# State advance of the running sequences placed between the convolution's matmul units, with four state buffers and the state transfers on GpSimd's queue

## The chip, the cores and the metric

The kernel runs on one core of one Trainium2 chip. The metric is the device time of one execution in microseconds (us), the median of the runs shown. One core has five engines with a queue each: PE (TensorE, matmuls), DVE (VectorE), ACT (ScalarE), POOL (GpSimd) and SP (SyncE, which here only starts transfers). They are ordered among each other by semaphores alone. The kernel is written without a scheduler: each engine executes its own hand-written list, and an instruction that waits for a semaphore holds up everything behind it on its engine.

## The reference

One step of a hybrid decoder layer, in float32: RMSNorm, a wide projection (`xn @ w_in`), two mixers side by side, sigmoid gates, an output projection, and a mixture of experts with a final RMSNorm. It runs for a new prompt of 512 tokens (`SEQ`) and for 8 running sequences (`DB`) of 8 new tokens each, 64 tokens (`ND`), 576 tokens in all (`T`).

One mixer is a short convolution of width 3 over `cc * ch`, multiplied by `cb`. The other is gated linear attention (GLA) with 4 heads (`H`), key width 128 and value width 256: `S = diag(a_t) S + k_t^T v_t`, `o_t = q_t S`. The prompt starts at a zero state. Each running sequence has a state of its own, `state_gla`, 4 x 128 x 256 floats, 512 KB: it is read, used for the sequence's 8 outputs, advanced by its 8 tokens, and returned in `gla_sample_new`. "State advance" below means this.

## The kernel before, in words

Every large matrix product is done in three passes of half-width floats (high times high, high times low, low times high). A weight group of 1 MB is loaded by SP into one of two buffers `raw`, copied by ACT to `wh` (`high`, line 703), and DVE computes the rest `wl` (`low`, line 1040). PE then works it off in units. A feature unit (`feature_unit`, matmuls at line 1585) is 48 matmuls of 288 columns and fills one of two pairs of PSUM banks; ACT or DVE empties a pair and signals `unit_free`. Groups are numbered: 8 to 11 gate the GLA output and are interleaved with the prompt's four GLA blocks, 12 to 17 (`G_CONV` to `G_GA`) are the convolution's, 18 to 21 and 22 to 25 the sigmoid gates (stage GA, then GB). Each convolution group has two units, twelve in all. A group's load waits until the low part of the group two before it is done; its `high` waits until PE has used up that group (`w_used`).

Behind the fourth GLA block of the prompt come the running sequences. PE transposes their keys (line 1696) and makes the scores (1698). It waits for ACT's copy of the keys (`kt`, line 836, behind the prompt's last `normed_output`), adds the scores' part of the output in banks 6 and 7 (line 1704), and then, sequence by sequence, does two things:

- the output's part from the state: 4 heads `qm x s0` (line 1710), when the state has been loaded (`st_load`);
- the state's increment: 4 heads `ksm x v` (line 1718) into banks 4 and 5, when POOL has masked the keys of this sequence (`km_ready`, line 568) and DVE has used the increment before (`st_ready`).

DVE computes the new state from the old one and the increment, in place (line 1235, 4 instructions). SP stores it (439) and, when the store has landed, loads the state of three sequences later into the same buffer (442): there are three buffers, `s0a`, `s0b` and `S`, the last of which also holds the prompt's state. SP's list has all of this ahead of the weight loads from group 14 on. When all is done, ACT normalises the outputs of the running sequences (`normed_output(NPT)`: four squares at line 809, POOL's power at 572 to 574, four scalings at 807). Only then do ACT and DVE go to the convolution: ACT copies `cc` (849), DVE multiplies by `ch` into `up` and `ud` (1253 to 1255), applies the taps (1263 to 1267), multiplies by `cb` (1277) and splits the result (1281). PE's list has the convolution's twelve units directly behind the last increment.

## Time and profile before

| | before |
|---|---|
| runs | 1057.36, 1057.85, 1051.64 us |
| median | 1057.36 us |
| span of the profiled execution, first to last instruction | 1039.5 us |
| PE busy | 900.2 us, 87% of the span |
| DVE, ACT, POOL busy | 53%, 43%, 21% |
| mean granted clock of PE | 0.928 of full speed |
| chain of work that ended last | PE 66%, DMA 12%, DVE 7%, POOL 5%, ACT 4% |

The page gives the profiled execution's span and no other time of it; the span is 17.9 us below the median of the runs, which includes what lies before the first and behind the last instruction. Full speed of PE is 2.4 GHz and the other level 1.2 GHz: a granted clock of 1.00 is the first, 0.50 the second, and a value between them is a mean over a stretch with both. Times of rows are microseconds from the span's start. A busy PE is not a PE at its peak.

### The profile page before, as it was taken

To read this page: it belongs to the slowest core of one execution; us is meant where nothing else is said; L and a number is where in the kernel's file an instruction comes from. 1 tells how busy PE (TensorE), PEld (TensorE's weight loads), DVE (VectorE), ACT (ScalarE), POOL (GpSimd) and SP (SyncE) were. 2 spreads that over 40 slices of the span, in tenths; PEclk is the share of its full clock that TensorE was granted. 3 is DMA by queue.
4 is the path that set the end of the run, shared out by engine and by line. 5 is a ranking of instruction groups with operands and counts; after the bars stand their busy time and mean duration, and the time that the engine had idled before them with its cause. 6 is when DMAs were issued, how large, how long until landed. Compare 5 with 4: busy or idle time off the path is not lost.

```text
span 1039.5 us, 16432 instructions
## 1 busy us (share of the span) xinstructions
PE 900.2 (87%) x6334; PEld 846.3 (81%) x6334; DVE 547.9 (53%) x695; ACT 446.5 (43%) x556; POOL 220.6 (21%) x286
## 2 busy tenths in 40 slices
PE   4999989998899999999998996269899989989950
PEld 3998988996589999999998996268888888878840
DVE  5413324655315431114654234647878878878737
ACT  5324323453021133223222124047778777778732
POOL 2000000001300000000000015215455454454533
PEclk9899989998999999999998996579999999999985
DMA  7222211112552222222434513169999999999526
GB/s 221 82 81 82 61 61 41 42 41 82 172 172 82 81 82 81 83 81 82 148 106 134 190 62 129 64 229 318 356 348 361 339 350 350 356 327 338 188 66 224
DMA packets 135535, 173.91 MB, mean 167 GB/s; under 512 B 10579, under 2 KB 120659, under 8 KB 134917
## 3 DMA queue, kind: packets, MB, share of 16 engines
q1 hardware_dynamic: 129556, 161.51, 46.7%
q0 software_dynamic: 5936, 11.81, 3.3%
q8 instruction: 30, 0.49, 0.2%
q14 instruction: 13, 0.10, 0.0%
HBM read 163.29 MB, written 17.86 MB: 174 GB/s over the span
## 4 chain that ended last, share of the span: by engine, by line
PE 66%; DMA 12%; DVE 7%; POOL 5%; ACT 4%; issue 4%; POOLq 0%; SPq 0%; ACTq 0%; DVEq 0%
PE ps L1585 51%; DMA xg<-moe_rows,curs 9%; PE ps L1845 5%; POOL curs L621 2%; DVE wl L1379 1%; ACT yb L955 1%; PE ps L1836 1%; PE ps L1675 1%; PE ps L1710 1%; POOL curd L634 1%; DMA xin<-x_sample 1%; DMA gla_sample_new<-s0b 1%; DMA s0b<-state_gla 1%; PE ps L1718 1%; PE ps L1689 1%
## 5 line engine op out<-in xcount | busy, mean ns | idle before, releaser
L1379 DVE TENSOR_TENSOR wl<-raw,wh 128x2048 fp32r<-128x2048 f32 x90 | 203.1, 2282 | 1.1 <-ACT wh L917 1.1
L1040 DVE TENSOR_TENSOR wl<-raw,wh 128x2048 fp32r<-128x2048 f32 x36 | 82.9, 2302 | 200.6 <-ACT wh L703 200.5
L1585 PE MATMUL ps<-xh,wh 128*128 128x288 f32 x832 | 180.7, 299 | 3.8 <-ACT hist L794 2.0
L1585 PE MATMUL ps<-xl,wh 128*128 128x288 f32 x832 | 179.3, 297 | 0.0
L1585 PE MATMUL ps<-xh,wl 128*128 128x288 f32 x832 | 179.3, 297 | 0.0
L917 ACT CAST wh<-raw 128x2048 fp32r<-128x2048 f32 x93 | 174.8, 1907 | 7.0 <-PE ps L1845 7.0
L1845 PE MATMUL ps<-wh,gx 128*128 128x256 f32 x512 | 140.3, 308 | 1.5 <-DVE gx L1483 1.5
L1585 PEld LDWEIGHTS ps<-xh,wh 128*128 128x128 f32 x832 | 135.3, 190 | 4.7 <-issue 2.3
L1585 PEld LDWEIGHTS ps<-xh,wl 128*128 128x128 f32 x832 | 135.2, 190 | 0.0
L1585 PEld LDWEIGHTS ps<-xl,wh 128*128 128x128 f32 x832 | 135.1, 190 | 0.0
L1845 PE MATMUL ps<-wl,gx 128*128 128x256 f32 x512 | 133.4, 295 | 0.0
L1845 PEld LDWEIGHTS ps<-wh,gx 128*128 128x128 f32 x512 | 104.5, 204 | 4.0 <-issue 1.7
L1845 PEld LDWEIGHTS ps<-wl,gx 128*128 128x128 f32 x512 | 104.8, 205 | 0.0
L703 ACT CAST wh<-raw 128x2048 fp32r<-128x2048 f32 x36 | 68.6, 1904 | 50.2 <-PE ps L1585 50.2
L556 POOL TENSOR_SCALAR ms<-ss 128x1 f32<-128x1 f32 (+2 forms) x19 | 7.3, 385 | 311.2 <-ACT v L809 230.4
L621 POOL COPY curs<-slots 64x1 int32 (+1 forms) x34 | 54.8, 1612 | 25.8 <-DVE slots L1461 19.4
L577 POOL IOTA io<- 128x160 f32 x1 | 0.3, 293 | 261.5 <-PE ps L1585 261.5
L634 POOL COPY curd<-slotd 64x1 int32 (+1 forms) x32 | 26.2, 819 | 127.5 <-ACT yb L955 127.5
L1585 PE MATMUL ps<-wh,xh 128*128 128x256 f32 x160 | 46.8, 293 | 6.6 <-ACT v L789 6.6
L1585 PE MATMUL ps<-wh,mh 128*128 128x256 f32 x160 | 46.7, 292 | 3.5 <-DVE ml L1339 3.5
L955 ACT COPY yb<-ps 64x1024 f32<-64x1024 f32 x32 | 32.2, 1007 | 35.2 <-PE ps L1585 35.2
L1585 PE MATMUL ps<-wl,mh 128*128 128x256 f32 x160 | 46.4, 290 | 0.0
(311 smaller groups left out, 1588.2 us busy)
## 6 DMA issues: line engine op xcount, KB each, us to landing
raw<-w_gate SPq DMA_DIRECT2D x32, 1024.0 KB, 6.3
raw<-w_up SPq DMA_DIRECT2D x31, 1024.0 KB, 7.7
raw<-w_down SPq DMA_DIRECT2D x30, 1024.0 KB, 7.6
raw<-w_in SPq DMA_DIRECT2D x26, 1024.0 KB, 5.1
raw<-w_gla_out SPq DMA_DIRECT2D x4, 1024.0 KB, 4.8
raw<-w_o SPq DMA_DIRECT2D x4, 1024.0 KB, 4.9
y<-moe_results SPq DMA_DIRECT2D x4, 1024.0 KB, 8.1
xin<-x_prompt SPq DMA_DIRECT2D x4, 512.0 KB, 6.5
```

The lines of the kernel that those rows point to most:

```text
L621: c(pool.tensor_copy(curs[p][:, :], slots[:, bass.ds(e, 1)]))
L634: c(pool.tensor_copy(curd[p][:, :], slotd[:, bass.ds(e, 1)]))
L703: copy(wh[par][:, :], raw[par][:, :]).then_inc(hi_ready, 1)
L917: copy(wh[m0 % 3][:, :], src[:, :]).then_inc(hi_ready, 1)
L955: copy(yb[e0 % 2][:, :].rearrange("p (a c) -> p a c", a=2), ps[0:B, 2:4, :]).then_inc(yb_ready, 1)
L1040: tt(wl[par][:, :], raw[par][:, :], wh[par][:, :].bitcast(F32), ALU.subtract).then_inc(lo_ready, 1)
L1379: tt(wl[m0 % 3][:, :], (raw[(m0 + 2) % 6] if m0 < NX else rawx[m0 - NX])[:, :], wh[m0 % 3][:, :].bitcast(F32), ALU.subtract).then_inc(lo_r ...
L1585: last.append(mm(out, left(a, k), right(b, k, o), start=k == 0 and n == 0, stop=k == k_tiles - 1 and n == 2))
L1675: ins = mm(ps[0:w, TB, q0:q0 + CH], kiv[:, hd, off:off + w], ql[:, hd, CH * n:CH * (n + 1)], start=True, stop=True)
L1689: ins = mm(ps[:, TB + hd // 2, (hd % 2) * DV:(hd % 2 + 1) * DV], kt[:, hd, :], v[:, j, hd * DV:(hd + 1) * DV], start=True, stop=True)
L1710: ins = mm(ps[0:ND, UB + hd // 2, (hd % 2) * DV:(hd % 2 + 1) * DV], qm[:, s, hd, :], s0[s % 3][:, hd, :], start=False, stop=s == DB - 1, s ...
L1845: ins = mm(ps[:, bank, 0:DE], gx[p][:, k, :], w[a][:, k, :], start=k == 0 and a == 0, stop=k == KD - 1 and a == 1)
```

## The change

The state advance is no longer a stage of its own. On PE the part from the scores is issued behind the first convolution unit, and the state advance of sequence s behind unit s + 2 (counted from 1), so that one stands behind each of the units 2 to 9. DVE's updates are spread over its convolution work in the same manner. ACT's `normed_output(NPT)` moves behind the convolution. There are four state buffers, in places that are free by then, and `up`, `ud` and `cs` are moved. The sixteen state transfers leave SP's queue and go to POOL's, between its maskings of the keys; SP's next weight load stands directly behind the store of the prompt's state.

```diff
+NS0 = 4
...
-        s0 = [sb("s0a", [P, H, DV], at=zone_b - 4 * H * DV), sb("s0b", [P, H, DV], at=zone_z + 4 * H * DV), S]
+        s0 = [sb("s0a", [P, H, DV], at=s1 + 4 * H * P), sb("s0b", [P, H, DV], at=zone_b - 4 * H * DV), S,
+              sb("s0d", [P, H, DV], at=qg_at)]
...
-        up = sb("up", [P, H, SEQ + 2])
         assert place[0] <= zone_b
+        up = sb("up", [P, H, SEQ + 2], at=zone_a)
         ud = sb("ud", [P, H, DB, DS + 2])
-        cs = sb("cs", [P, H, 2 + 2 * DB])
-        assert place[0] <= zone_b
+        assert place[0] <= s1
...
@@ block.sync
             sp.wait_ge(s_ready, NPT + 1)
             sp.dma_start(gla_prompt_new[0, 0].rearrange("h d v -> d h v"), S[:, :, :]).then_inc(out_done, 16)
-            for s in range(2):
-                if s == 0:
-                    sp.wait_ge(sg_ready, 2 * NPT + 1)
-                sp.dma_start(s0[s][:, :, :], st_in[s]).then_inc(st_load[s], 16)
-            sp.wait_ge(out_done, 16)
-            sp.dma_start(s0[2][:, :, :], st_in[2]).then_inc(st_load[2], 16)
-            for s in range(DB):
-                sp.wait_ge(st_ready, s + 1)
-                sp.dma_start(st_out[s], s0[s % 3][:, :, :]).then_inc(st_store, 16)
-                if s + 3 < DB:
-                    sp.wait_ge(st_store, 16 * (s + 1))
-                    sp.dma_start(s0[s % 3][:, :, :], st_in[s + 3]).then_inc(st_load[s % 3], 16)
             for g in range(G_CONV + 2, G_GA):
@@ block.gpsimd
-            pool.wait_ge(kt_ready, NPT + 1)
-            for s in range(DB):
+            def state_in(s):
+                pool.dma_start(s0[s % NS0][:, :, :], st_in[s]).then_inc(st_load[s % NS0], 16)
+
+            def state_out(s):
+                pool.wait_ge(st_ready, s + 1)
+                pool.dma_start(st_out[s], s0[s % NS0][:, :, :]).then_inc(st_store, 16)
+
+            def one_sequence(s):
                 if s >= 2:
                     pool.wait_ge(dkv_full, s - 1)
                 pool.tensor_scalar(ksm[s % 2][0:ND, :, :], kt[0:ND, :, :], inseq[:, s:s + 1], None,
                                    ALU.mult).then_inc(km_ready, 1)
+            pool.wait_ge(scans_done, NPT + 1)
+            state_in(0)
+            pool.wait_ge(s_ready, NPT + 1)
+            pool.wait_ge(sg_ready, 2 * NPT + 1)
+            state_in(1)
+            pool.wait_ge(out_done, 16)
+            state_in(2)
+            pool.wait_ge(kt_ready, NPT + 1)
+            one_sequence(0)
+            one_sequence(1)
+            pool.wait_ge(p1_full, NPT + 1)
+            pool.wait_ge(gla_in, NPT + 2)
+            state_in(3)
+            for s in range(DB):
+                state_out(s)
+                if s + 2 < DB:
+                    one_sequence(s + 2)
+                if s + NS0 < DB:
+                    pool.wait_ge(st_store, 16 * (s + 1))
+                    state_in(s + NS0)
...
@@ block.scalar
-            act.wait_ge(o_full, 1)
-            act.wait_ge(dkv_full, DB)
-            normed_output(NPT)
-
-            act.wait_ge(st_store, 16 * DB)
+            act.wait_ge(sg_ready, 2 * NPT + 1)
             for t in range(2):
...
+            act.wait_ge(o_full, 1)
+            normed_output(NPT)
+            act.wait_ge(cs_ready, 1)
+            act.wait_ge(st_store, 16 * DB)
             for g0, base, dst in ((G_GA, U_GA, m1), (G_GB, U_GB, sgb)):
@@ block.vector
-            for s in range(DB):
+            def state_update(s):
                 dve.wait_ge(dkv_full, s + 1)
-                dve.wait_ge(st_load[s % 3], 16 * (s // 3 + 1))
+                dve.wait_ge(st_load[s % NS0], 16 * (s // NS0 + 1))
...
-            dve.wait_ge(st_store, 16 * DB)
-            dve.wait_ge(o_full, 1)
             c(dve.memset(up[:, :, 0:2], 0.0))
             c(dve.tensor_copy(ud[:, :, :, 0:2], hist[:, :, :].rearrange("p c (s w) -> p c s w", w=2)))
+            state_update(0)
             for t in range(2):
...
                         low((g0 + 1) % 2, (g0 + 1) // 2 + 1)
+                    if t == 0:
+                        state_update(u + 1)
+                    elif u == 0:
+                        state_update(7)
...
                     tt(zl[:, ct, :], tmp[u][:, :], zh[:, ct, :].bitcast(F32), ALU.subtract).then_inc(z_ready, 1)
+                    if t == 0:
+                        state_update(u + 3)
                 low((g0 + 2) % 2, (g0 + 2) // 2 + 1)
+                if t == 0:
+                    state_update(5)
+                    state_update(6)
@@ block.tensor
+            def decode_scores():
                 ...
+            def decode_state(s):
                 ...
             for g in range(G_CONV, G_GA):
                 pe.wait_ge(lo_ready, g + 1)
                 for u in range(2):
                     free(u, N_CONV // 2 + g - G_CONV)
                     feature_unit(g % 2, u, u, X).then_inc(w_used if u else unit_full, 1)
+                    n = 2 * (g - G_CONV) + u
+                    if n == 0:
+                        decode_scores()
+                    elif n <= DB:
+                        decode_state(n - 1)
```

The bodies of `decode_scores` and `decode_state` are the instructions that stood ahead of the convolution, with the buffer number taken modulo 4 instead of 3; `decode_scores` ends with the wait for `gla_in` that stood ahead of the states.

PE's list, from the scores of the running sequences on, before (`sc`, `qm`, `bc`, `ec` are the scores, the queries of one sequence, and the two buffers of masked keys):

```order
L1698 MATMUL ps<-qg_120,ql 64x64 x4
L1704 MATMUL ps<-v,sc 64x256 [waits on_ready,sc_ready,kt_ready]
L1704 MATMUL ps<-v,sc 64x256 x3
L1710 MATMUL ps<-s0a,qm 64x256 [waits st_load0,gla_in]
L1710 MATMUL ps<-s0a,qm 64x256 x3
L1718 MATMUL ps<-v,bc 128x256 [waits km_ready]
L1718 MATMUL ps<-v,bc 128x256 x3
L1710 MATMUL ps<-s0b,qm 64x256 [waits st_load1]
L1710 MATMUL ps<-s0b,qm 64x256 x3
L1718 MATMUL ps<-v,ec 128x256 [waits st_ready,km_ready]
L1718 MATMUL ps<-v,ec 128x256 x3
```

All sequences stand one behind the other, and the first convolution unit (line 1585) comes behind the eighth.

The end of the first convolution unit, the scores' part, and the start of the second unit in PE's list now (line numbers are those of the changed kernel: 1611 is the unit, 1731 the scores' part):

```order
L1611 MATMUL ps<-xh,wl_83 128x288 x2
L1731 MATMUL ps<-v,sc 64x256 [waits on_ready,sc_ready,kt_ready]
L1731 MATMUL ps<-v,sc 64x256 x3
L1611 MATMUL ps<-xh,wh_81 128x288 [waits unit_free1,gla_in]
L1611 MATMUL ps<-xh,wh_81 128x288
L1611 MATMUL ps<-xl,wh_81 128x288 x2
```

The end of the second unit, the first sequence, and the start of the third unit now (1738 and 1746 are the former 1710 and 1718):

```order
L1611 MATMUL ps<-xl,wh_81 128x288 x2
L1611 MATMUL ps<-xh,wl_83 128x288 x2
L1738 MATMUL ps<-s0a,qm 64x256 [waits st_load0]
L1738 MATMUL ps<-s0a,qm 64x256 x3
L1746 MATMUL ps<-v,bc 128x256 [waits km_ready]
L1746 MATMUL ps<-v,bc 128x256 x3
L1611 MATMUL ps<-xh,wh_82 128x288 [waits unit_free0,lo_ready]
L1611 MATMUL ps<-xh,wh_82 128x288
L1611 MATMUL ps<-xl,wh_82 128x288 x2
L1611 MATMUL ps<-xh,wl_84 128x288 x2
```

Between two sequences there is now always one unit of 48 matmuls; the waits in front of the instructions are the same ones.

SP's list before, from the store of the prompt's state:

```order
L430 DMA gla_prompt_new<-S 128x4x256 [waits s_ready]
L434 DMA s0a<-state_gla 128x4x256 [waits sg_ready]
L434 DMA s0b<-state_gla 128x4x256
L436 DMA S<-state_gla 128x4x256 [waits out_done]
L439 DMA gla_sample_new<-s0a 128x4x256 [waits st_ready]
L442 DMA s0a<-state_gla 128x4x256 [waits st_store]
L439 DMA gla_sample_new<-s0b 128x4x256 [waits st_ready]
L442 DMA s0b<-state_gla 128x4x256 [waits st_store]
```

All but the first of these rows, and nine more like them, are gone from SP's list. POOL's list at the same place of the program now (556 loads, 560 stores, 565 masks the keys):

```order
L556 DMA s0a<-state_gla 128x4x256 [waits scans_done]
L556 DMA s0b<-state_gla 128x4x256 [waits sg_ready,s_ready]
L556 DMA S<-state_gla 128x4x256 [waits out_done]
L565 TENSOR_SCALAR bc<-kt,inseq 64x512 [waits kt_ready]
L565 TENSOR_SCALAR ec<-kt,inseq 64x512
L556 DMA s0d<-state_gla 128x4x256 [waits gla_in,p1_full]
L560 DMA gla_sample_new<-s0a 128x4x256 [waits st_ready]
L565 TENSOR_SCALAR bc<-kt,inseq 64x512 [waits dkv_full]
L556 DMA s0a<-state_gla 128x4x256 [waits st_store]
L560 DMA gla_sample_new<-s0b 128x4x256 [waits st_ready]
L565 TENSOR_SCALAR ec<-kt,inseq 64x512 [waits dkv_full]
L556 DMA s0b<-state_gla 128x4x256 [waits st_store]
```

A store, a masking and a load of a later sequence take turns, each with its wait, on one queue.

## Rows read from the trace of the kernel before

**Rows 1.** Bounds, length; busy PE, PEld, DVE, ACT, POOL; granted clock, DMA share, GB/s.
```profile
247.00:295.00 48.00, 39.89 (x150) 23.70 (x148) 16.59 (x35) 5.39 (x14) 13.66 (x10) 0.86 0.55 173
295.00:372.00 77.00, 77.00 (x578) 76.91 (x578) 31.77 (x56) 16.94 (x24) 1.22 (x2) 1.00 0.33 104
```

**Rows 2.** The chain of waits in the state advance: start, length, what.
```profile
252.47 3.67 PE ps L1704 x8
...
260.95 1.87 PE ps L1710 x8
...
275.07 3.55 PE ps L1710 x8
...
293.24 1.92 PE ps L1718 x8
```

**Rows 3.** Waits of PE from 225 to 480: total, times, longest.
```profile
PE ps L1710 <- DMA s0a<-state_gla: 2.1, 2, 1.5
PE ps L1710 <- DMA s0b<-state_gla: 2.0, 1, 2.0
```

**Rows 4.** PE's timeline: start, length, instruction, in brackets idle time before it.
```profile
249.22 0.60 PE L1696 MATMUL ps<-ident,kst 128*64 128x128 f32 x4 [1.84 <-DVE S L1215]
249.75 0.68 PE L1698 MATMUL ps<-qg,ql 128*64 128x64 f32 x8
...
285.86 3.42 PE L1710 MATMUL ps<-s0a,qm 128*64 128x256 f32 x8 [1.48 <-DMA s0a<-state_gla]
```

**Rows 5.** ACT's timeline: outputs normalised, first convolution unit emptied, first two of GA.
```profile
295.26 0.38 ACT L809 ACTIVATE v<-ps 64x256 f32<-64x256 f32 x1 [41.05 <-PE ps L1718]
...
298.23 1.55 ACT L807 ACTIVATE v<-ps,rs 64x256 f32<-64x256 f32 x4 [1.42 <-POOL rs L574]
...
301.84 0.64 ACT L849 COPY tmp<-ps 128x576 f32<-128x576 f32 x1 [2.06 <-PE ps L1585]
...
378.66 1.28 ACT L696 ACT_TABLE_LOAD   x1 [3.20 <-PE ps L1585]
...
385.07 0.20 ACT L696 ACTIVATE gnh<-gnh 128x1 f32<-128x1 f32 x1 [2.94 <-PE ps L1585]
```

**Rows 6.** The chain of waits among GLA blocks: units of 48 matmuls.
```profile
205.17 6.38 PE ps L1585 x48
...
214.63 6.47 PE ps L1585 x48
```

**Rows 7.** Busy time and granted clock in three short stretches, columns as in rows 1.
```profile
252.00:258.00 6.00, 5.53 (x13) 2.79 (x14) 2.66 (x1) 2.21 (x2) 3.12 (x2) 0.50 0.73 247
274.00:280.00 6.00, 4.92 (x15) 2.85 (x16) 0.72 (x2) 0.00 (x0) 0.68 (x1) 0.72 0.58 178
506.00:508.00 2.00, 0.39 (x3) 0.15 (x2) 1.42 (x3) 1.81 (x2) 0.00 (x0) 1.00 0.00 0
```

**Rows 8.** DVE's timeline: a convolution unit's first step, its low part, a state update.
```profile
314.66 0.46 DVE L1253 TENSOR_TENSOR up<-ps,tmp 128x288 f32<-128x288 f32 x1 [13.21 <-PE ps L1585]
...
318.30 2.29 DVE L1040 TENSOR_TENSOR wl<-raw,wh 128x2048 fp32r<-128x2048 f32 x1
...
291.24 1.65 DVE L1235 SCALAR_TENSOR_TENSOR s0a<-s0a,eb,ps 128x256 f32<-128x256 f32 x4 [5.17 <-PE ps L1718]
```

**Rows 9.** POOL's transfers: durations in ns (min/median/max) and landing; masking the keys.
```profile
L624 POOL DMA_INDIRECT xg<-moe_rows,curs x34: 955/967/1080, 675.0 to 995.5; - x34
L600 POOL DMA_DIRECT2D moe_rows<-x x5: 533/600/827, 620.2 to 633.5; - x5
...
DMA to landing us min/median/max: 2.9/3.1/5.5
...
261.05 1.56 POOL L568 TENSOR_SCALAR bc<-kt,inseq 64x512 f32<-64x512 f32 x1 [5.41 <-PE ps L1718]
```

**Rows 10.** POOL's timeline: the same power alone, and beside DVE's work.
```profile
622.59 0.56 POOL L558 TENSOR_TENSOR rs<-ms,expo 128x1 f32<-128x1 f32 x1
...
626.78 1.49 POOL L558 TENSOR_TENSOR rs<-ms,expo 128x1 f32<-128x1 f32 x1
```

More of the change, by code:

```diff
@@ L198, in build @@
         ec = sb("ec", [P, H, P])
+        qg_at = place[0]
         qg0 = sb("qg0", [P, H, P])
@@ L221, in build @@
         sgb = sb("sgb", [P, KD, T])
-        up = sb("up", [P, H, SEQ + 2])
         assert place[0] <= zone_b
+        up = sb("up", [P, H, SEQ + 2], at=zone_a)
         ud = sb("ud", [P, H, DB, DS + 2])
-        cs = sb("cs", [P, H, 2 + 2 * DB])
-        assert place[0] <= zone_b
+        assert place[0] <= s1
         h = sb("h", [P, NT, D], at=zone_v + 2 * 4 * KD * TP)
         tmp = [sb(f"tmp{i}", [P, T]) for i in range(2)]
+        cs = sb("cs", [P, H, 2 + 2 * DB])
         cso = sb("cso", [2 + 2 * DB, DC], at=zone_a + 2 * 4 * KD * T)
@@ L316, in build @@
         g_act, sg_ready = sem("g_act"), sem("sg_ready")
-        st_load = [sem(f"st_load{i}") for i in range(3)]
+        st_load = [sem(f"st_load{i}") for i in range(NS0)]
         st_store, km_ready, dkv_full, st_ready = (sem(n) for n in ("st_store", "km_ready", "dkv_full", "st_ready"))
@@ L1230, in _ @@
             low((NPT - 1) % 2, (NPT - 1) // 2 + (G_G // 2 + 1))
-            for s in range(DB):
+            def state_update(s):
                 dve.wait_ge(dkv_full, s + 1)
-                dve.wait_ge(st_load[s % 3], 16 * (s // 3 + 1))
+                dve.wait_ge(st_load[s % NS0], 16 * (s // NS0 + 1))
                 for hd in range(H):
-                    ins = stt(s0[s % 3][:, hd, :], s0[s % 3][:, hd, :], eb[:, hd, s * DS + DS - 1:s * DS + DS],
+                    ins = stt(s0[s % NS0][:, hd, :], s0[s % NS0][:, hd, :], eb[:, hd, s * DS + DS - 1:s * DS + DS],
                               ps[:, TB + hd // 2, (hd % 2) * DV:(hd % 2 + 1) * DV], ALU.mult, ALU.add)
@@ L1699, in _ @@
             ins.then_inc(p1_full, 1)
-            pe.wait_ge(kt_ready, NPT + 1)
-            pe.wait_ge(sc_ready, NPT + 1)
-            pe.wait_ge(on_ready, NPT + 1)
-            for hd in range(H):
-                mm(ps[0:ND, UB + hd // 2, (hd % 2) * DV:(hd % 2 + 1) * DV], sc[0:ND, hd, 0:ND],
-                   v[0:ND, NPT, hd * DV:(hd + 1) * DV], start=hd % 2 == 0, stop=False, skip_group_check=True)
-            pe.wait_ge(gla_in, NPT + 2)
-            for s in range(DB):
-                pe.wait_ge(st_load[s % 3], 16 * (s // 3 + 1))
+            def decode_scores():
+                pe.wait_ge(kt_ready, NPT + 1)
+                pe.wait_ge(sc_ready, NPT + 1)
+                pe.wait_ge(on_ready, NPT + 1)
+                for hd in range(H):
+                    mm(ps[0:ND, UB + hd // 2, (hd % 2) * DV:(hd % 2 + 1) * DV], sc[0:ND, hd, 0:ND],
+                       v[0:ND, NPT, hd * DV:(hd + 1) * DV], start=hd % 2 == 0, stop=False, skip_group_check=True)
+                pe.wait_ge(gla_in, NPT + 2)
+            def decode_state(s):
+                pe.wait_ge(st_load[s % NS0], 16 * (s // NS0 + 1))
                 for hd in range(H):
                     ins = mm(ps[0:ND, UB + hd // 2, (hd % 2) * DV:(hd % 2 + 1) * DV], qm[:, s, hd, :],
-                             s0[s % 3][:, hd, :], start=False, stop=s == DB - 1, skip_group_check=True)
+                             s0[s % NS0][:, hd, :], start=False, stop=s == DB - 1, skip_group_check=True)
                 if s == DB - 1:
```

## The prediction

> **What bounds the kernel here.** I read first the chain of waits of the whole execution: PE's work is 66% of it, so a change pays only where PE stands still or runs slowly. The table by stages then shows where that is near the change. In the 48 us of the state advance PE is busy 39.9 us at a mean granted clock of 0.86, although nothing in it is a large product; in the 77 us of the convolution PE is busy all the time at 1.00, DVE for 31.8 us, ACT for 16.9, POOL for 1.2, and the DMA engines a third of the time [rows 1]. The first stage is bound by waits, the second by PE with every other engine in hand.
>
> The chain of waits inside the first stage says which ones. The eight matmuls on one state take 1.87 us and the eight of its increment 1.92 when nothing is amiss; but another eight on a state take 3.55 [rows 2]. PE waited there for the loads of states, 2.0 us once and 2.1 us in two times [rows 3], and its timeline shows a second slow eight, 3.42 us, right behind an idle time of 1.48 us that ended with a load [rows 4]. So a late state costs twice, by the wait and by the lower clock level (1.2 GHz in place of 2.4) behind it. From 252 to 258 the clock stands at 0.50 without a break, and from 274 to 280 at 0.72 in the mean, that is (1 - 0.72) x 6 / 0.5 = 3.4 us at the lower level [rows 7].
>
> **What PE no longer waits for.** PE ends the scores of the running sequences at 249.75 + 0.68 = 250.43 [rows 4] and begins the first convolution unit when the last increment ends, 293.24 + 1.92 = 295.16 [rows 2]. From the first unit's copy at 301.84 to the same point of the first GA unit at 378.66 [rows 5] there are twelve units: 76.82 / 12 = 6.40 us each. The convolution thus ends at 295.16 + 76.8 = 371.96.
>
> In the changed list the first unit can start at 250.43: its weights were split during the third GLA block, and its pair of banks is free. Behind it PE has, without waits and at full clock:
>
> - twelve units, 12 x 6.40 = 76.8 us;
> - the scores' part, eight matmuls of the increment's shape but half its rows, 1.92 (it took 3.67 at the lower clock [rows 2]);
> - eight sequences, 8 x (1.87 + 1.92) = 30.3 us;
> - nine returns from small matmuls to a unit. A GLA block's unit behind small score matmuls takes 6.47 us against 6.38 behind the large ones [rows 6]: 9 x 0.09 = 0.8 us.
>
> That is 109.8 us and an end at 360.2, 11.7 us earlier than 371.96. Nothing is computed less: the 11.7 us are PE's idle time and its slow matmuls.
>
> **The gap that stays.** PE still stands for 1.84 us before it transposes the keys, since that waits for DVE's update of the prompt's state [rows 4]. Does the clock fall behind it? Gaps of 2.0 us [rows 3] and 1.48 us [rows 4] were followed by slow matmuls; from 506 to 508 PE was busy for 0.39 us of 2 and the clock stayed at 1.00 [rows 7]. In the execution shown it was at 0.50 from 252 on, though a second wait lay there too. The bounds are nothing and the 6 us of 252 to 258; matmuls there go at 1.87 / 3.55 of their speed, so it costs 6 x (1 - 0.53) = 2.8 us. I take the shorter spell, 3.4 us and 3.4 x 0.47 = 1.6, since the first slow stretch before began behind this very gap. The sum is then 11.7 - 1.6 = 10.1 us.
>
> **DVE.** It now waits for an increment between two convolution steps, and what is queued behind that wait is the next unit's evacuation and the next low part; PE waits for both. A unit costs DVE 318.30 - 314.66 = 3.64 us of steps, 2.29 for a low part and 1.65 for a state update [rows 8], 7.6 us, while PE takes 6.40 + 3.79 = 10.2 for a unit and a sequence. The tightest place is the third update, behind the low part of group 15, which cannot begin before PE has ended the fourth unit: it is done some 7.6 us after that, and PE wants it for the fourth sequence's increment 3.79 + 6.40 + 1.87 = 12.1 us after it. Cost nothing, 4.5 us in hand; were the cover gone, each late update would hold PE by its lateness.
>
> **ACT.** The final `normed_output` takes 298.23 + 1.55 - 295.26 = 4.52 us and now stands between the last `high` of the convolution and the first GA unit, where ACT was idle for 3.20 us [rows 5]. That unit's evacuation is 1.3 us later than before, when ACT was done with it 2.94 us ahead of the end of the second GA unit, at which PE wants the banks [rows 5]. Cost nothing, 1.6 us in hand, of which a POOL power stretched as in [rows 10] (0.56 to 1.49) takes 0.9.
>
> **SP and POOL.** SP loses sixteen transfers and its next weight load is issued early; in the convolution PE waited for none [rows 1]. POOL gains them, and the trace has no direct transfer of 512 rows on POOL's queue. Its five transfers of up to 128 rows took 0.53 to 0.83 us of POOL's time, 0.60 in the median, and landed after 2.9 to 5.5 us; the gathers, whose rows are found by an index, took 0.97 for 64 rows [rows 9]. Lower bound 0.53 (rows cost nothing); four times the median, 2.4; from the gathers, 8 x 0.967 = 7.7. I take 2.4, because the direct transfers are the same kind of instruction. POOL's share of a sequence is then two transfers and a masking of 1.56 [rows 9], 6.4 us of PE's 10.2. It decides only above (10.2 - 1.56) / 2 = 4.3 us in the steady run, and at the beginning (three loads and a masking before PE wants the first masked keys, two units, the scores' part and eight matmuls after 250.43, at 267.1) above 5.0. A buffer's store and reload, 2.4 + 5.5 + 2.4 + 5.5, need 16 us of the four sequences, 41 us, after which it comes up again. In bytes, 8 MB over 110 us join 104 GB/s at a DMA share of 0.33 [rows 1]: hidden.
>
> Here a rule speaks against the change. POOL's own work does stretch beside DVE's, 0.56 to 1.49 us for the same power [rows 10]. The Trainium skill (SBUF — State Buffer, Summary: rules for kernel authors) says that a transfer from GpSimd's queue, to be hidden under DVE, should go through SP's or ACT's, since its descriptors cannot be written while DVE runs in its faster modes. No row of this trace shows that for a transfer. If each transfer waited out a low part, POOL's price would be 2.4 + 2.29 = 4.7 us; its fourteen transfers and eight maskings up to the last masked keys would be done 14 x 4.7 + 12.5 = 78 us after 250.43, at 329, and PE wants them nine units, the scores' part, seven sequences and eight matmuls after 250.43, 57.6 + 1.9 + 26.5 + 1.9 and 0.8 for the returns, at 339. The sum stands, but the fourth case below gains chance.
>
> **Sum.** The transfers, DVE and ACT lie beside PE, so 10.1 us remain. The trace has a span of 1039.5 us, 17.9 under the median of the runs; what lies around the span is not touched, and behind the convolution everything is released by PE's progress and moves forward as a whole. From the median, 1057.36 - 10.1 = 1047.3 us. The runs themselves spread over 6.2 us, and 1% (10.6 us, an end below 1046.8) is about what a measurement of this kernel can tell from no change.
>
> **Four cases.**
>
> 1. As summed, with one slow spell behind the remaining gap: 1047.3 us, chance 0.47.
> 2. The clock stays up: 11.7 us, 1045.7, chance 0.33. For it speaks the stretch at 506, against it that the work between the gap and the first unit is 1.2 us of small matmuls.
> 3. The change does not do what it says: PE still meets late states or keys. With the waits for loads as before, 2.0 + 2.1 us [rows 3], and two slow spells of 1.6 us, 7.3 of the 11.7 us come back: 1057.4 - 4.4 = 1053. Against it stand 10.2 us per sequence in place of 3.8 and a fourth buffer. Chance 0.13.
> 4. POOL becomes the bound and the kernel slower. Above 4.3 us per transfer it begins to hold PE; at 6.3 the last masked keys come 11.7 us late and all is lost; at the gathers' 7.7 they come at 250.43 + 14 x 7.7 + 12.5 = 371 in place of 339, 32 us late, and the time is 1057.4 + 32 - 11.7 = 1077. For it speak the rows four times as many and [rows 10], against it that 128 rows cost no more than 0.83. Chance 0.07.
>
> Case 1 lies 0.5 us on the near side of 1% and the runs' spread puts about 0.36 of it beyond, of case 2 about 0.72: faster by over 1% 0.47 x 0.36 + 0.33 x 0.72 = 0.41; slower 0.07; within 1% the rest, 0.52. The range takes in cases 1 and 2 with the spread of the runs on the low side and case 3 on the high side: 1041 to 1054.
>
> **What would show it.** In the new trace the stage of the state advance is gone; the first convolution unit starts about 250.4, units stand 10.2 us apart with 3.8 us of state matmuls between them, each group of eight at 1.9 us, and the first GA unit is emptied about 10 us earlier than 378.66 (a little more for ACT's part). A slow spell, if there is one, shows as a clock of 0.50 for some 3.4 us inside the first unit or two. DVE's updates come before PE's increments, POOL's transfers take under 4.3 us each, and PE's idle time inside the convolution is near zero. The prediction is wrong if PE waits there for POOL's masked keys or for a state's load, if the second GA group waits for ACT, or if the time won is given back in the expert stage.

## The result and the profile after

The changed kernel took 1037.73 us, the median of four runs (1034.48 to 1040.51), against 1054.53 us for four runs of the kernel before (1051.64 to 1057.85): a ratio of 0.9868, 95% interval 0.9822 to 0.9914. It is faster, by 0.9 to 1.8%, and the time is lower than forecast: 1047.3 us was predicted, and it lies below the range of 1041 to 1054. Here and below, executions more than 1.5% above the fastest of the same kernel beside them are left out of medians, means, ratios and spreads: ten of the kernel before (nine from 1055.63 to 1063.50 us, one of 1492.86), three of the version with the order undone (1057.14 to 1063.08) and one of that with a second gap (2559.44).

The chain of waits of the changed kernel (start, length, what) takes the place of [rows 2]:

```profile
247.06 1.67 DVE S L1233 x4
248.72 0.14 issue
248.86 0.60 PE ps L1722 x4
249.46 0.61 PE ps L1724 x8
250.06 6.58 PE ps L1611 x48
256.64 1.87 PE ps L1731 x8
258.51 6.58 PE ps L1611 x48
265.09 1.87 PE ps L1738 x8
266.96 1.92 PE ps L1746 x8
268.88 6.59 PE ps L1611 x48
275.48 1.87 PE ps L1738 x8
277.35 1.92 PE ps L1746 x8
```

L1722 and L1724 transpose the decode keys and form the scores, L1611 is a convolution unit, L1731 the scores' product, L1738 a state's and L1746 its increment's. Nothing but PE is in this chain behind DVE's update of S: units of 6.6 us and sequences of 3.79 us alternate, 10.4 us apart, and every eight take 1.87 or 1.92 us. The eights of 3.67 and 3.55 us are gone. The waits of PE from 225 to 480 us (in total, times, longest), beside [rows 3]:

```profile
PE ps L1722 <- DVE S L1233: 1.8, 1, 1.8
PE ps L1783 <- DVE tmp L1328: 1.3, 1, 1.3
```

No load of a state and no masked key is among them; the second row lies near 470 us, behind the GA and GB units, where the kernel before has the same wait (1.3 us near 480), and is not of this stage. The table by stages (length, busy time of PE, PEld, DVE, ACT and POOL, granted clock, DMA share, GB/s), beside [rows 1, 7]:

```profile
247.00:295.00 48.00, 46.16 (x301) 40.27 (x301) 21.03 (x41) 10.37 (x18) 16.25 (x16) 1.00 0.52 175
252.00:258.00 6.00, 6.00 (x42) 5.34 (x42) 2.43 (x3) 2.49 (x3) 5.40 (x4) 1.00 1.02 372
...
274.00:280.00 6.00, 6.00 (x34) 4.47 (x33) 4.21 (x10) 0.00 (x0) 0.80 (x1) 1.00 0.30 90
295.00:360.00 65.00, 65.00 (x420) 57.34 (x419) 26.55 (x50) 8.81 (x8) 12.31 (x11) 1.00 0.35 122
```

PE is busy for 46.16 of the 48 us that held the state advance before, and all that is missing is the 1.84 us in which it waits for S. The clock stays at 1.00 behind that gap. POOL's groups from 240 to 372 us (busy time, mean ns of one, idle time before), beside [rows 9, 10]:

```profile
L565 POOL TENSOR_SCALAR ec<-kt,inseq 64x512 f32<-64x512 f32 x4 | 7.5, 1866 | 0.1
L565 POOL TENSOR_SCALAR bc<-kt,inseq 64x512 f32<-64x512 f32 x4 | 7.3, 1816 | 0.1
L556 POOL DMA_DIRECT2D s0a<-state_gla x2 | 1.8, 910 | 1.2 <-DMA gla_sample_new<-s0a 1.2
...
L560 POOL DMA_DIRECT2D gla_sample_new<-S x2 | 1.6, 786 | 12.8 <-DVE S L1253 12.8
```

A transfer of 512 rows costs POOL 0.76 to 0.91 us in the mean, not 2.4.

To compare executions I use one stretch: from the end of the last key-value product (row of L1715 in the chain, L1689 in the kernel before) to the first transpose of the convolution's state. It is 423.2 - 247.38 = 175.8 us before and 412.0 - 247.02 = 165.0 after:

```profile
L1740 PE MATMUL ps<-ident,cs x4: 273/273/273, 423.2 to 423.5; 128*18 128x128 f32 x4
```

```profile
L1773 PE MATMUL ps<-ident,cs x4: 272/272/273, 412.0 to 412.3; 128*18 128x128 f32 x4
```

These are the groups by line of PE in the kernel before and in the changed one (durations, first and last start). The stage thus gave 10.8 us, between the 10.1 us of case 1 and the 11.7 of case 2, though the time fell 9.6 us lower than forecast. The stage cannot be where the forecast failed by that much. Nor can the work right behind it: from the convolution's state to the first result of the experts it is 701.7 - 423.2 = 278.5 us before and 690.6 - 412.0 = 278.6 after.

### The profile page after: what moved, and what is told of

It reads as the page before. It is cut to its first block, busy times and chain, and to the rows that moved or that the text cites. A ratio compares the mean times of both kernels' runs of the same rounds, so it can differ in the third digit from the quotient of the medians.

```text
span 1032.7 us, 16433 instructions
## 1 busy us (share of the span) xinstructions
PE 898.4 (87%) x6334; PEld 846.5 (82%) x6334; DVE 546.8 (53%) x695; ACT 446.3 (43%) x556; POOL 234.8 (23%) x302
## 4 chain that ended last, share of the span: by engine, by line
PE 68%; DMA 11%; DVE 7%; POOL 6%; ACT 4%; issue 3%; POOLq 0%; SPq 0%; ACTq 0%; DVEq 0%
PE ps L1611 52%; DMA xg<-moe_rows,curs 9%; PE ps L1878 5%; POOL curs L639 2%; PE ps L1746 1%; PE ps L1738 1%; ACT yb L973 1%; PE ps L1869 1%; POOL moe_results L655 1%; DVE wl L1405 1%; PE ps L1701 1%; POOL curd L652 1%; DMA xin<-x_sample 1%; POOL ms L542 1%; PE ps L1715 1%
## 5 line engine op out<-in xcount | busy, mean ns | idle before, releaser
L1611 PE MATMUL ps<-xh,wh 128*128 128x288 f32 x832 | 181.6, 300 | 3.8 <-ACT hist L812 2.0
L1611 PE MATMUL ps<-xh,wl 128*128 128x288 f32 x832 | 179.2, 297 | 0.0
L1611 PE MATMUL ps<-xl,wh 128*128 128x288 f32 x832 | 179.2, 297 | 0.0
L1611 PEld LDWEIGHTS ps<-xh,wh 128*128 128x128 f32 x832 | 134.9, 190 | 7.5 <-issue 5.1
L1611 PEld LDWEIGHTS ps<-xh,wl 128*128 128x128 f32 x832 | 135.2, 190 | 0.0
L1611 PEld LDWEIGHTS ps<-xl,wh 128*128 128x128 f32 x832 | 135.1, 190 | 0.0
L1611 PE MATMUL ps<-wh,xh 128*128 128x256 f32 x160 | 46.7, 292 | 6.6 <-ACT v L807 6.6
L1611 PE MATMUL ps<-wh,mh 128*128 128x256 f32 x160 | 46.7, 292 | 3.5 <-DVE ml L1365 3.5
L1611 PE MATMUL ps<-wh,hh 128*128 128x512 f32 x128 | 43.3, 420 | 3.9 <-DVE wl L1405 2.4
L1611 PE MATMUL ps<-wl,mh 128*128 128x256 f32 x160 | 46.5, 290 | 0.0
```

The costliest lines, as they stand in the source:

```text
L1611: last.append(mm(out, left(a, k), right(b, k, o), start=k == 0 and n == 0, stop=k == k_tiles - 1 and n == 2))
```

## Experiments

The edits are against the changed kernel, except for the first. All runs of one comparison were made on one chip with runs of the kernel before.

**The base.** The kernel before, unchanged.

> The kernel before, unchanged, run again. What is open is the base of the prediction's sum: it took the 17.9 us between the profiled span (1039.5) and the median (1057.4) for time that lies around the span. Theory: only about 1.8 us lie around it, as in the four runs of the changed kernel (span 1032.7, time 1034.48), and the runs of the kernel before differ inside the span, between about 1041 and 1058; the profiled execution was simply a short one, and the differing time is spent behind the convolution, in the experts. Every run's time less its span is then 1.8 +- 0.3. Rival: the kernel before really has 12 to 18 us around its span, which the changed kernel does not have; time less span is 10 us or more. Ratio to the kernel before: 1.000 +- 0.006 either way.

Measured: 12 runs, median 1051.45 us (1042.49 to 1056.17), ratio 1.0002 (0.9965 to 1.0039). Its spans are 1.7 to 1.9 us below the times in every run, and so they are in all the 28 runs of the kernel before that stood beside it. One of these has a span of 1039.5 us, as long as the profile shown before, and a time of 1041.22. So the theory holds: hardly anything lies around the span, and the profiled execution, whose own time is not on record, must have been a short one of about 1041.3 us. All comparisons but the first together use 71 runs of the kernel before, from 1039.51 to 1056.62 us, median 1049.95.

Where the runs differ is seen in two profiles of the same kernel. This one's group of the experts' result copies (durations in ns, first and last start):

```profile
L955 ACT COPY yb<-ps x32: 1006/1007/1009, 702.9 to 1011.3; 64x1024 f32<-64x1024 f32 x32
```

and the same group in the first profile of the kernel before:

```profile
L955 ACT COPY yb<-ps x32: 1006/1007/1009, 701.7 to 1003.2; 64x1024 f32<-64x1024 f32 x32
```

The stretch up to the convolution's state is 175.7 us here against 175.8 there, but from the first to the last result it is 308.4 us against 301.5. In between, this execution has a granted clock of 0.94 against 0.96 and PE waits 23.5 us for gathered rows against 21.3. All fourteen profiles of the study have this stretch between 300.5 and 312.0 us, and the three of the changed kernel alone between 304.5 and 307.9.

**More runs of the changed kernel**, in two comparisons.

> The changed kernel, unchanged, with more runs. Theory: the convolution ends 11.2 us earlier than in the kernel before in every profile (near 361 us), PE runs at a granted clock of 1.00 through 250 to 360 us with the 1.8 us gap ahead of it, and the time is 10 to 15 us below the kernel before run beside it (ratio 0.986 to 0.991). Rival (the prediction's likeliest case): the gap calls for the clock's lower level in other executions, and the gain at the convolution's end is then 9.6 us or less.

> The changed kernel beside it once more. Theory: stretch 165.0 us, median near 1037 us, ratio to the kernel before 0.987 to 0.991; time less span 1.8 us in each run. Rival: the ratio lies at 0.985 or below, as the first four runs had it, and the gain is then above the 10.8 us of the stage.

Measured: ratios 0.9895 (0.9860 to 0.9930, 11 runs, median 1037.21) and 0.9887 (0.9831 to 0.9943, 6 runs, median 1039.12). The stretch is 165.0 us both times, to 0.1 us what it was in the first profile, and no slow spell lies in it. All 21 runs have a mean of 1038.2 us against 1049.25 for the 71 of the kernel before: 11.0 us, +- 1.7 by their spread. The first four runs of each side had shown 16.8 between medians. So the gain is near the 10.1 us forecast, and it was the level of both times that was forecast too high.

**The order alone undone.** All states ahead of the convolution, with four buffers and POOL's queue:

```diff
+            decode_scores()
+            for s in range(DB):
+                decode_state(s)
             for g in range(G_CONV, G_GA):
...
-                    if n == 0:
-                        decode_scores()
-                    elif n <= DB:
-                        decode_state(n - 1)
```

(and DVE's eight updates in a row ahead of its convolution steps)

> The changed kernel with the interleaving alone undone: four buffers, transfers on GpSimd's queue, all eight sequences ahead of the convolution as in the kernel before. Theory: the order of PE's work makes the gain, so almost all 11.2 us at the convolution's end are lost, and as GpSimd waits for each store to land before it loads again, a sequence takes 0.8 + 3.5 + 0.9 = 5.2 us there against PE's 3.8 and the stage comes out up to 6 us longer: the convolution ends at 370 to 378 us, the time is 1041 to 1062 us, ratio to the kernel before 0.996 to 1.008. Rival: the fourth buffer and the other queue make half the gain or more by themselves, and the convolution ends at 366 us or earlier.

Measured: median 1045.33 us of nine runs, ratio 0.9984 (0.9944 to 1.0024), stretch 425.1 - 248.65 = 176.5 us. All of the gain is lost, so it belongs to the order of PE's and DVE's work, as the theory says. Whether three buffers would do in the new order was not tried. The waits of PE from 225 to 440 us show what took the loads' place:

```profile
PE ps L1738 <- POOL bc L565: 2.1, 2, 1.6
PE ps L1738 <- POOL ec L565: 2.1, 1, 2.1
PE ps L1723 <- ACT kt L854: 2.0, 1, 2.0
PE ps L1714 <- DVE S L1233: 1.8, 1, 1.8
PE ps L1730 <- DMA s0a<-state_gla: 1.3, 1, 1.3
```

With 3.8 us to a sequence POOL's masks, queued behind its waits for landed stores, come late by 4.2 us in all. This is the wait of case 4 in a milder form; 10.4 us to a sequence cover it.

**The transfers on SP's queue**, each load and store between the loads of the convolution's weights:

```diff
...
             for g in range(G_CONV + 2, G_GA):
                 sp.wait_ge(lo_ready, g - 1)
                 load(g % 2, win[:, :, conv[g - G_CONV]:conv[g - G_CONV] + 256])
+                k = g - (G_CONV + 2)
+                for s in range(2 * k, 2 * k + 2):
+                    state_out(s)
...
```

(`state_in` and `state_out` move from POOL to SP, and `state_out` there also loads the state of four sequences later)

> The changed kernel with the 16 state transfers on the SP engine's queue again, between the loads of the convolution's weights; four buffers, order of PE and DVE as changed. Theory: with 10.4 us to a sequence either queue is early enough, and the choice of the queue is worth nothing: the stretch from the last key-value product to the transposes of the convolution's state stays at 165.0 +- 0.3 us. Rival: SP waits for each store to land before it goes on to the next weight group, the loads of groups come late, PE waits at units 7 to 11, and the stretch is 168 us or longer.

Measured: ratio 0.9918 (0.9880 to 0.9956), median 1039.49, stretch 412.6 - 247.35 = 165.3 us, with one new wait of PE of 0.2 us for DVE's update. For the stage either queue will do. The theory's last word, "nothing", is too much: see the last experiment.

**POOL made dearer.** Each transfer in 8 and in 16 parts, `state_in` and `state_out` issuing pieces of a head:

```diff
-                pool.dma_start(s0[s % NS0][:, :, :], st_in[s]).then_inc(st_load[s % NS0], 16)
+                for hd in range(H):
+                    for a in range(0, DV, 128):
+                        pool.dma_start(s0[s % NS0][:, hd, a:a + 128], st_in[s][:, hd, a:a + 128]
+                                       ).then_inc(st_load[s % NS0], 16)
...
```

> The changed kernel with each state transfer issued in 8 parts (128 rows of 512 bytes each) on GpSimd's queue, to raise GpSimd's time per transfer from 0.8 us to about 4.4 us (8 x 0.55). The prediction's case 4 put the point at which GpSimd begins to hold PE at 4.3 us in the steady part. Theory (the sum over GpSimd's order: store, mask, wait for the store's landing, load): the sixth and seventh masks come 0.6 and 2 us late, the stretch from the last key-value product to the transposes of the convolution's state is 165 to 169 us. Rival: transfers by GpSimd beside DVE's work cost much more than their descriptors, and the stretch passes 172 us.

> As before in 16 parts (128 rows of 256 bytes each), about 8.8 us of GpSimd per transfer, twice what it can spare. Theory: GpSimd is the bound, the eighth mask comes about 38 us late, and the stretch is 165 + 30 to 45 = 195 to 210 us, the time near 1075 us, as the prediction's case 4 worked out for a price of 7.7 us. Rival: the parts are issued faster than 0.55 us each, and the stretch stays under 180 us.

Measured: 1041.06 us, one run, stretch 165.0 us with 8 parts; 1088.78 us and 463.6 - 247.98 = 215.6 us with 16. The loads of the first (durations in ns, minimum, median, maximum; first and last start):

```profile
L558 POOL DMA_DIRECT2D s0a<-state_gla x16: 544/544/798, 248.0 to 280.4; - x16
L558 POOL DMA_DIRECT2D s0b<-state_gla x16: 544/544/592, 252.6 to 291.6; - x16
```

8 x 0.544 = 4.4 us per transfer, at the edge from which case 4 was to decide (4.3 by the prediction, (10.4 - 1.57) / 2 = 4.4 with the 10.4 us that a unit and a sequence take), holds nothing: PE's only wait is that for S, and the sixth and seventh masks, expected 0.6 and 2 us late, held up nothing. With 16 parts a transfer takes 8.7 us, and PE waits for masks (from 225 to 440 us):

```profile
PE ps L1752 <- POOL bc L571: 22.5, 3, 10.8
PE ps L1752 <- POOL ec L571: 10.6, 2, 6.1
PE ps L1728 <- DVE S L1239: 1.8, 1, 1.8
```

That is 33.1 us of waits, but the stretch grew by 50.6, more than the 30 to 45 expected. The table by stages has the rest:

```profile
258.00:290.00 32.00, 21.21 (x116) 18.15 (x115) 1.66 (x4) 2.77 (x3) 31.96 (x57) 0.79 0.32 88
290.00:360.00 70.00, 53.54 (x274) 44.43 (x273) 23.33 (x43) 5.68 (x5) 66.53 (x117) 0.84 0.33 99
```

POOL is busy almost throughout, and PE's clock, 1.00 in the changed kernel, is 0.79 and 0.84 in the mean: each of the five waits, 4.47 to 10.79 us long and with 13 us or more of work between them, brought a slow stretch behind it. The eight behind each takes 3.78 us in place of 1.92, and the unit behind the last of them 8.34 in place of 6.59, together 3.6 us more; five times that is 18, and 33.1 + 18 = 51 is the growth measured. Case 4's mechanism exists; the kernel is far from it at 0.8 us per transfer.

**A second gap next to the first.** The scores' product ahead of the first unit:

```diff
...
+            decode_scores()
             for g in range(G_CONV, G_GA):
...
-                    if n == 0:
-                        decode_scores()
-                    elif n <= DB:
+                    if 1 <= n <= DB:
                         decode_state(n - 1)
```

> The changed kernel with the decode scores' product put back ahead of the first convolution unit, so that PE's second gap (2.0 us, for ACT's copy of the keys) returns right behind the first of 1.8 us; the states stay between the units. Measured from the end of the last key-value product to the transposes of the convolution's state, a stretch of 175.8 us before and 165.0 us after the change. Theory (the two gaps together bring the clock's lower level, one alone does not): the stretch is 165.0 + 2.0 for the wait + 1.6 to 4.4 for a slow spell at 0.50 = 168.6 to 171.4 us. Rival: the clock stays at 1.00 through this gap too, and the stretch is 167.0 us; the spells of the kernel before then came from its small matmuls, not from the gaps.

Measured: ratio 0.9992 (0.9949 to 1.0035), median 1042.84 of nine runs, stretch 419.5 - 248.48 = 171.0 us, so 6.0 us more than the changed kernel: 2.0 of wait and 4.2 of a slow spell, less 0.2 for one return to a unit fewer. PE's timeline (start, length, instruction, idle time before) and two rows of the table by stages:

```profile
250.32 0.60 PE L1722 MATMUL ps<-ident,kst 128*64 128x128 f32 x4 [1.84 <-DVE S L1233]
250.85 0.68 PE L1724 MATMUL ps<-qg,ql 128*64 128x64 f32 x8
253.56 3.67 PE L1731 MATMUL ps<-v,sc 64*64 64x256 f32 x8 [2.03 <-ACT kt L854]
257.16 0.85 PE L1611 MATMUL ps<-xh,wh 128*128 128x288 f32 x2
257.81 0.68 PE L1611 MATMUL ps<-xl,wh 128*128 128x288 f32 x2
```

```profile
252.00:258.00 6.00, 4.44 (x11) 2.48 (x12) 2.50 (x4) 3.31 (x5) 5.17 (x5) 0.53 1.01 344
258.00:264.00 6.00, 6.00 (x32) 6.00 (x31) 0.00 (x0) 0.00 (x0) 1.87 (x2) 0.62 0.99 350
```

The eight products take 3.67 us, 1.80 more than 1.87, and the next two units take 15.37 us in the chain, 2.4 more than 6.58 and 6.40; the granted clock is 0.53 from 252 to 258 us and 0.62 from 258 to 264. In slices of half a microsecond it is 1.00 up to 252.0, falls inside the second gap (0.84 from 252.0 to 252.5) and is back near 1.00 from 262.5 on. This is the slow spell of [rows 2, 4, 7] again, from a kernel that has the rest of the change: the second gap brought it back, and the rival's 167.0 us is out.

A rule for the clock does not follow from this, neither that two gaps are needed nor that one between large units is harmless. In the kernel before, the gap of 1.48 us in [rows 4] stands alone, 9.3 us behind the one before it, and the clock fell (0.87 in the gap, 0.50 in the two microseconds behind it). And a later wait, 1.8 to 1.9 us for DVE's tile `xl` between two units, stands in all fourteen profiles: the clock fell behind it in six of them and stayed at 1.00 in eight. First the changed kernel, in which it stayed, PE's row and then a stretch behind it (columns as above):

```profile
497.02 0.52 PE L1611 MATMUL ps<-xh,wh 128*128 128x288 f32 x2 [1.79 <-DVE xl L1341]
```

```profile
499.00:501.00 2.00, 2.00 (x17) 2.00 (x17) 1.56 (x3) 0.00 (x0) 0.00 (x0) 1.00 0.13 15
```

and the version with the transfers on SP's queue, in which it fell:

```profile
497.61 0.53 PE L1608 MATMUL ps<-xh,wh 128*128 128x288 f32 x2 [1.79 <-DVE xl L1338]
```

```profile
499.60:501.60 2.00, 2.00 (x10) 2.00 (x9) 1.56 (x3) 0.00 (x0) 0.00 (x0) 0.50 0.14 16
```

So the same gap between the same matmuls brings the lower level in some executions and not in others; what decides it is open. The gap of 1.84 us for S with units behind it left the clock at 1.00 in all six profiles that have it.

**The gap for S filled.** The first unit ahead of the transposes (which move into a function `decode_keys`), scores behind the second, states behind the third to the tenth (DVE's updates one unit later):

```diff
...
                     if n == 0:
+                        decode_keys()
+                    elif n == 1:
                         decode_scores()
-                    elif n <= DB:
-                        decode_state(n - 1)
+                    elif n <= DB + 1:
+                        decode_state(n - 2)
```

> The changed kernel with its first convolution unit put ahead of the transposes of the decode keys, scores behind the second unit and states behind the third to the tenth. Theory: PE's last gap ahead of the convolution, 1.8 us in which it waits for DVE's update of S, is filled by the unit, which needs nothing of S, and nothing else becomes late: the convolution ends 1.8 us earlier than in the changed kernel (about 359 us), the time 1.5 to 2 us lower, 0.998 of the changed kernel. Rival: the scores' inputs come 6.6 us later, and PE meets a wait of about 2 us for them or for the second weight group's low part, which DVE makes behind the masked scores; the end stays at 361 us.

> The version with the first unit ahead of the transposes again, with more runs beside the changed kernel on the same chip. Theory: its stretch is 163.0 us against 165.0, and its time 2 us below the changed kernel's, about 1035 us median, ratio to the kernel before 0.986 to 0.988. Rival: the 2 us are given back in the experts, where executions differ by 8 us, and the times cannot be told from the changed kernel's.

Measured: ratios 0.9862 (0.9809 to 0.9914) and 0.9891 (0.9833 to 0.9948), medians 1034.82 and 1037.89, stretch 163.0 us both times. PE meets no wait at all between 225 and 440 us, and its chain runs on:

```profile
246.81 1.73 PE ps L1711 x8
248.54 6.37 PE ps L1607 x48
254.91 0.44 PE ps L1719 x4
255.35 0.61 PE ps L1721 x8
255.96 6.59 PE ps L1607 x48
```

The gain of 2.0 us, 1.84 for the gap and 0.2 because the first unit stands right behind the key-value product (6.37 against 6.58), is the same in both profiles' stretch and cannot be told in the times, for which the experts' 300 to 312 us are too unsteady.

**The second gap alone.** As the version above, but with the scores' product right behind the keys and the states where the changed kernel has them:

```diff
...
                     if n == 0:
+                        decode_keys()
                         decode_scores()
```

> The first convolution unit ahead of the transposes of the decode keys (which fills the gap of 1.8 us), then the keys and right behind them the scores' product, so that the gap of 2.0 us for ACT's copy of the keys stands alone, behind a full unit; states behind the units 2 to 9 as in the changed kernel. Theory (a lone gap of 2 us leaves the clock at 1.00, two of them close together with little work between bring the lower level): the stretch from the last key-value product to the first of the transposes of the convolution's state is 163.0, as with the unit first, + 2.0 for the wait - 0.2 for one return to a unit less = 164.8 us, clock 1.00 throughout. Rival (any such gap with small products around it brings the lower level, as in the variant with the scores ahead, where the spell took 4.0 us): 168 to 169 us with a window of 0.5 to 0.7 behind the gap.

Measured: ratio 0.9863 (0.9793 to 0.9933), median 1035.85, stretch 163.5 us, clock 1.00. But PE's only wait there is 0.7 us, not 2.0: while the unit ran, ACT had finished the norms of the last block, which stand ahead of its copy of the keys. The experiment missed its question. The wait for `xl` above, which brought the lower level in this very profile, is the nearest answer that the profiles have: a lone gap does not always leave the clock up.

**Both gains.** The first unit ahead, and SP's queue:

> The first unit ahead of the transposes, with the state transfers on the SP engine's queue. In the profiles so far the span ends 6.1 us behind the issue of the last output's store where the 16 state transfers are on GpSimd's queue, and 4.8 us behind it where they are on SP's. Theory: that tail goes with the queue, and the two gains add: stretch from the last key-value product to the first of the transposes of the convolution's state 163.0 to 163.4 us, tail 4.8 us, the time 3 us below the changed kernel's, ratio to the kernel before 0.985 to 0.988. Rival: the tail has another cause, and it is 6.1 us here too; or SP's order (weights, stores, loads) now holds PE, and the stretch is 165 us or longer.

The edit joins the two above; state 7's update on DVE stands ahead of the low part that followed it. Measured: median 1032.31 us, ratio 0.9839 (0.9792 to 0.9886), just below the 0.985 to 0.988 expected, stretch 163.3 us with two new waits of PE of 0.4 and 0.3 us; the lowest median of all versions. SP's last store (issue, length) and the span, here:

```profile
core 0 of [0], span 1033.4 us
...
1028.58 0.52 SPq L382 DMA_DIRECT2D y_sample<-yo  x1
```

and in the changed kernel:

```profile
core 0 of [0], span 1032.7 us
...
1026.61 0.52 SPq L382 DMA_DIRECT2D y_sample<-yo  x1
```

and, with a span of 1039.5 us, in the kernel before:

```profile
1034.68 0.52 SPq L379 DMA_DIRECT2D y_sample<-yo  x1
```

The tail is 4.8 us here, as in the kernel before, and 6.1 in the changed kernel: the sixteen transfers on POOL's queue cost 1.3 us at the very end, which no term of the prediction had. Both pairs of versions that differ in the queue, with the first unit ahead and without, show the same step. Against the changed kernel this version gains 1.7 us in the stretch and 1.3 in the tail; the intervals of the two ratios still overlap.

## Why the prediction missed

**The step that failed is the base of the sum**, "From the median, 1057.36", with its reason, "17.9 under the median of the runs; what lies around the span is not touched". It took the difference between the profiled span and a median of three runs for time outside the span. In every run whose span is on record that is 1.7 to 1.9 us; the rest was the spread of the executions, most of it, in the two profiles compared, in the experts. Two of the three runs (1057.36 and 1057.85 us) are longer than all of the 71 later ones that count (1039.5 to 1056.6), and the profile lies at their short end. With the median of the 71, 1049.95, the same sum gives 1039.9. The profiled execution alone would have been no better a base: 1039.5 + 1.8 - 10.1 = 1031.2.

Of the 9.6 us between 1047.3 and 1037.73, the base is 7.4. The gain of the stage, 10.8 instead of 10.1, is 0.7, and it is near by two errors of opposite sign (the spell that did not come, the returns, both below). The tail works the other way by 1.3. The 2.8 us that remain include 0.9 by which the first four runs lie under the median of all 21 (1038.6); the other 1.9 are about the uncertainty of 1.7 between the two means, and I do not assign them.

By its other steps:

- **What PE no longer waits for: right.** The loads' waits, the scores' wait and all slow eights are gone, and it is the order that does it, as the order undone shows.
- **The gap that stays: its 1.6 us were not spent.** The gap of 1.84 us is there, but the clock stays up in all three profiles of the changed kernel, so case 2 describes it. Two readings behind this term were wrong. The first slow stretch before did not begin behind this gap but inside the second one: the clock is 1.00 up to 251.0 us, 0.85 in the half microsecond from there and 0.50 behind it. And the stretch at 506, taken as a sign that the clock stays up, is the wait for `xl`, behind which the clock fell in six of fourteen profiles. So no row told cases 1 and 2 apart, and a choice between them was a guess.
- **Returns to a unit: too small.** 0.09 us was taken from a GLA block's unit behind small matmuls [rows 6]; a unit behind the state's matmuls takes 6.59 against 6.40, so 0.19. Nine of them are 0.9 us more, which is the difference between the 10.8 us of the stage and 11.7.
- **DVE and ACT: right.** No wait of PE for either inside the convolution, nor in the GA units. ACT's norm began at 364.20 and ended at 369.37, 5.2 us in place of 4.5, since POOL's part was stretched as allowed for; 1.6 us in hand were enough.
- **POOL: right that it is hidden, price three times too high.** 0.76 to 0.91 us per transfer against 2.4. Rows cost little: 512 of them came near the 128 of [rows 9]. The Trainium skill's warning (SBUF — State Buffer, Summary: rules for kernel authors) that transfers from GpSimd's queue are held up while DVE runs in its faster modes cost nothing here: with 8 parts, the eight loads from 276.54 us on, during which DVE worked without a break, took 4.35 us together, 0.544 each like the others. Whether DVE ran in one of the modes that the rule speaks of, no row says.
- **Cases 3 and 4.** No wait for a state or a key occurred inside the convolution, and POOL held nothing up.

## What to carry to other kernels

Before a time is predicted from a span, ask whether the profiled execution is a typical one: compare span and time of the same execution, and take the spread of several runs as the uncertainty of the base, above all where a late stage waits for gathers. A short gap of PE can cost more than its length: here 3.9 us of two gaps with little work between brought 4.2 us of lower clock as well. But the gap of 1.8 us for `xl` brought it in some executions and not in others, so read more than one profile before a forecast counts on either. Interleaving a latency-bound chain with large products paid here although it added 0.19 us for each return, and it made the choice of the queue and even a fivefold issue cost irrelevant to the stage, because the period per step grew from 3.8 to 10.4 us.

## What was not expected of the hardware

- The execution's end depends on the transfers on POOL's queue. From the issue of the last store to the end of the span it is 4.8 us without state transfers on it (four profiles), 6.1 with 16 (eight), 8.7 with 128 (8 parts), but 4.8 again with 256 (16 parts). No instruction shows in that time, and the cause is open.
- The same program's executions spread over 17 us (the 71 above), most of it, where two profiles show it, between the experts' first and last result (6.9 of 8.1 us), with more waits for gathered rows and a lower mean clock in the longer one. Which of the two comes first was not tried.
- The same wait of PE, 1.8 to 1.9 us between two units, was followed by a clock of 0.50 in six of fourteen profiles and by 1.00 in eight.
- Longer waits cost more than themselves each time: 33.1 us of five waits for masks made the stretch 50.6 us longer, with a clock of 0.79 to 0.84 in place of 1.00.
